# Gate projections of a hybrid decoder layer as three products of hi and lo parts, in 64 filler pieces

## The chip, the core and the metric

One core of a Trainium2 chip runs the whole layer as one program. Its engines are TensorE (PE, with PEld for its weight loads), VectorE (DVE), ScalarE (ACT), GpSimd (POOL) and SyncE (SP, which here only issues DMAs). Each engine runs its own instructions strictly in the order in which they are written, and waits on semaphores for the others; an instruction that waits holds up all that stands behind it on its engine. The metric is the device time of one execution in microseconds, and lower is better.

## What is computed

Input x is 256 tokens by 2048, in fp32. The part of the reference that matters:

```python
h = rms_norm(x)
proj = einsum('btd,dc->btc', h, w_in)          # 2048 x (q,k,v | z | gates)
q, k, v, z, gates = split(proj, ...)           # gates: 2 * 2048 columns
attn = sliding_window_attention(q, k, v)       # 16 heads, 2 blocks of 128 queries
y = rwkv7(z)                                   # 16 heads, delta-rule recurrence
ga, gb = split(gates, (2048, 2048))
merged = sigmoid(ga) * (attn @ w_branch_a) + sigmoid(gb) * (y @ w_branch_b)
x = x + merged @ w_out
x = x + hierarchical_moe(rms_norm(x))          # 32 experts
out = rms_norm(x)
```

## The kernel before

The program runs through these stages: the z, q, k, v and low-rank projections; attention in four units (u = 0 to 3: query block u // 2, and one half of the heads); the recurrence in two halves (hh = 0, 1: eight heads each); the merge with w_branch_a and w_branch_b and the product with w_out; the experts.

The projections ahead of attention, and the merge and w_out behind the recurrence, split both operands. ACT copies a piece of 1024 weight columns into an fp32r buffer (hi), DVE subtracts it from the original (lo), and PE adds three fp32r products, hi by hi, hi by lo and lo by hi (`PRODUCTS`). The gates, 4096 columns of w_in from `GA0` on, are still plain fp32 products. They serve as fillers: PE runs a few of their k steps at places in attention and recurrence where it would wait for DVE or ACT.

`gate_mm(count)` runs the next `count` k steps. A k step multiplies 128 rows of hT by 512 gate columns for 128 tokens, and the compiler makes two PE instructions of it (L571). There are 16 x 16 = 256 of them, 16 for each tile of 128 tokens by 512 columns, and all tiles use PSUM bank 7. `gate_half()` is `gate_mm(8)`. ACT's `gate_out` takes the sigmoid of a finished tile (L1141) and stores it to DRAM (L1143); the next tile's first product waits for it.

The order on PE is written out by hand. Each attention unit has the scores (L595), k steps of the gates, a wait for DVE's softmax (`pr_done`), transposes (L470), 8 more k steps, a wait for ACT's copy of the transposes (`pt_done`, L1157) and the product with v (L615). ACT then copies the result (L1160, `pv_done`), and the next unit's scores wait for that. The four units hold 16, 16, 24 and 24 k steps.

In a half of the recurrence the order on PE is: w and a products (L640, L641, L644), cumulative sums (`cum`, L653), norms (`ks`, L660), transposes of v (`vtr`), bonus (`bon`, L674); then a wait for DVE's long chain up to `bon_done` (L1526 to L1539, with the reciprocal L1527); then L688 and L693 (`l`, `lt`), 8 k steps, L701 (`mt`), more transposes and L717, and five levels of a triangular inverse (L734, k steps, L753, L751). Behind the levels follow L759, the products f, g and rb (L773 to L782), the step between two chunks of the state (`s`, L807), the outputs (`yy`, L818), and the normalisation of y. k steps stand at nearly all of these places: 96 in the first half, 80 in the second.

`ring` has four slots of 2 MB. SP loads gate columns through `load()` into slots as they come free, and w_branch_a and w_branch_b behind them.

The core of the gates before, on PE:

```python
def gate_mm(count):
    for m in range(gate_part[0], gate_part[0] + count):
        tile, k = divmod(m, KT)
        ...
        if k == 0 and tile:
            pe.wait_ge(S("gate_out"), tile)
        if k % 8 == 0:
            full(n)
        last = mm(ps[:, 7, :], hT[:, k, 128 * t:128 * t + 128], slot(n)[:, k % 8, :],
                  start=k == 0, stop=k == KT - 1)
```

Of the kernel before, what the change touches and what calls it, by code (L numbers as in the profile page):

```python
# [4 lines left out]
F32 = mybir.dt.float32  # L5
# [6 lines left out]
P = 128  # L12
# [115 lines left out]
def hybrid_layer(nc, a, out):  # L128
    with ExitStack() as ctx:
# [9 lines left out]

        ring = sb("ring", [P, RING, SLOT])  # L140
# [22 lines left out]

        def over(stack, name, shape, dt=F32R):
            return stack.enter_context(nc.sbuf_tensor(name, shape, dt))

        with ExitStack() as early:
            over(early, "below_w", [P, 15104], F32)
            w3 = [over(early, f"w_{x}", [P, 3, 1024]) for x in ("hi", "lo")]
            w1 = [over(early, f"w4_{x}", [P, 1, 1024]) for x in ("hi", "lo")]  # L170
            over(early, "below_h", [P, 1024], F32)
            h_hi, h_lo = (over(early, f"h_{x}", [P, KT, TOK]) for x in ("hi", "lo"))
# [30 lines left out]
        hT = A(HT, 4096).rearrange("p (k t) -> p k t", k=KT)  # L203
# [59 lines left out]

        def late_pieces(b):

            return [v3[x][:, b, :] for x in range(2)]
# [3 lines left out]
        UZ, UQ, UL, UM, UO = 48, 24, 6, 32, 32  # L270
        BLOCKS = ((0, 0), (0, 1), (1, 0), (1, 1), (0, 2), (0, 3), (1, 2), (1, 3))
# [34 lines left out]
        NG = NL + 2  # L306
        NM = NG + 16
# [28 lines left out]
        def _(sp):  # L336
# [89 lines left out]
        def _(pool):  # L426
# [9 lines left out]
            pool.wait_ge(S("const_in"), 16)  # L436
            for hh in range(HALVES):
# [25 lines left out]
        def _(pe):  # L463
# [95 lines left out]
            def gate_mm(count):  # L559


                for m in range(gate_part[0], gate_part[0] + count):
                    tile, k = divmod(m, KT)
                    b, t = divmod(tile, TT)
                    n = NG + 2 * b + k // 8
                    if k == 0 and tile:

                        pe.wait_ge(S("gate_out"), tile)
                    if k % 8 == 0:
                        full(n)  # L570
                    last = mm(ps[:, 7, :], hT[:, k, 128 * t:128 * t + 128], slot(n)[:, k % 8, :],  # L571
                              start=k == 0, stop=k == KT - 1)
                    if t and k % 8 == 7:
                        last.then_inc(S("chunk_used"), 1)
                    elif k == KT - 1:
                        last.then_inc(S("gate_ps"), 1)
                gate_part[0] += count

            def gate_half():
                gate_mm(8)  # L580
# [7 lines left out]
            for u in range(4):  # L588
# [9 lines left out]
                gate_half()  # L598
                if u >= 2:
                    gate_half()  # L600
# [7 lines left out]
                gate_half()  # L608
# [19 lines left out]
            for hh in range(HALVES):  # L628
# [18 lines left out]
                if hh == 0:  # L647
                    gate_half()
# [6 lines left out]
                last.then_inc(S("half_ps"), 1)  # L655

# [5 lines left out]
                if hh == 0:  # L662
                    gate_half()
# [6 lines left out]
                gate_half()  # L670
# [5 lines left out]
                gate_half()  # L676
                gate_half()
# [18 lines left out]
                gate_half()  # L696
# [31 lines left out]
                for lv in range(1, 6):  # L728
# [8 lines left out]
                    gate_mm((3, 3, 3, 3, 4)[lv - 1])  # L737
# [46 lines left out]
                gate_half()  # L784
# [14 lines left out]
                for c in (1, 2):  # L799
# [10 lines left out]
                    if c == 1:  # L810
                        gate_half()
# [9 lines left out]
                gate_half()  # L821
                gate_half()
# [14 lines left out]
            assert gate_part[0] == 16 * KT  # L837
# [184 lines left out]
        def _(act):  # L1022
# [98 lines left out]
            gate_tile = [0]  # L1121
# [10 lines left out]
            def gate_out():  # L1132

                q = gate_tile[0]
                gate_tile[0] += 1
                b, t = divmod(q, 2)
# [721 lines left out]
```

## Time and profile before

| what | us |
|---|---|
| median of 3 runs | 1860.07 (1857.42 to 1862.98) |
| the profiled execution | 1861.89 |
| its span in the trace | 1860.0 |
| projections ahead of attention | 20 to 247 |
| attention | 247 to 347 |
| first half of the recurrence | 347 to 520 |
| second half of the recurrence | 520 to 693 |
| merge, w_out, router | 693 to 890 |
| experts | 890 to 1860 |

The span is what the trace covers; 1.9 us of the profiled execution lie around it. Times in the trace are microseconds from the start of the span. The rows on which the prediction rests stand below in groups, each with the view that it comes from. In a row of instructions in order of time the first number is the start and the second the duration; the bracket at its end is the engine's idle time ahead of it and what ended it. In a row of a stretch stand its start and end, its length, then busy time and count of instructions of PE, PEld, DVE, ACT and POOL, the mean granted clock as a share of full, the DMA share and GB/s. In a row of a group stand sum and mean (ns) of busy time, then the idle time ahead and what ended most of it.

### The profile page before, as it was taken

To read this page: it belongs to the slowest core of one execution; us is meant where nothing else is said; L and a number is where in the kernel's file an instruction comes from. 1 tells how busy PE (TensorE), PEld (TensorE's weight loads), DVE (VectorE), ACT (ScalarE), POOL (GpSimd) and SP (SyncE) were. 2 spreads that over 40 slices of the span, in tenths; PEclk is the share of its full clock that TensorE was granted. 3 is DMA by queue.
4 is the path that set the end of the run, shared out by engine and by line. 5 is a ranking of instruction groups with operands and counts; after the bars stand their busy time and mean duration, and the time that the engine had idled before them with its cause. 6 is when DMAs were issued, how large, how long until landed. Compare 5 with 4: busy or idle time off the path is not lost.

```text
span 1860.0 us, 24062 instructions
## 1 busy us (share of the span) xinstructions
PE 1454.8 (78%) x10818; PEld 834.8 (45%) x10818; DVE 503.5 (27%) x666; ACT 347.7 (19%) x399; POOL 37.3 (2%) x33
## 2 busy tenths in 40 slices
PE   7999999999989999998767567575575665765754
PEld 7999964447546758886312113122121221211311
DVE  5555444252253256644101001010010100100102
ACT  5444332311121134444101001000010000100001
POOL 1000000002001100000000000000000000000000
PEclk9999999899979999999869779788887888977887
DMA  9555424240202239555699999999999999999993
GB/s 355 189 180 181 143 96 147 95 147 21 97 33 76 99 123 331 196 226 203 274 421 422 422 422 422 422 422 422 422 422 421 422 422 421 422 422 421 423 422 146
DMA packets 114524, 529.04 MB, mean 284 GB/s; under 512 B 7408, under 2 KB 9722, under 8 KB 64410
## 3 DMA queue, kind: packets, MB, share of 16 engines
q1 hardware_dynamic: 109616, 514.50, 69.2%
q0 software_dynamic: 2048, 8.24, 1.2%
q10 hardware_dynamic: 2794, 5.31, 0.8%
q8 instruction: 55, 0.90, 0.2%
q14 instruction: 11, 0.09, 0.0%
HBM read 521.74 MB, written 6.29 MB: 284 GB/s over the span
## 4 chain that ended last, share of the span: by engine, by line
PE 57%; DMA 34%; DVE 4%; ACT 3%; issue 1%; ACTq 0%; DVEq 0%; SPq 0%; POOL 0%; POOLq 0%
DMA ring<-in_expert_w_down 17%; DMA ring<-in_expert_w_up 11%; PE ps L508 11%; PE ps L571 10%; PE ps L843 9%; PE ps L961 7%; DMA ring<-in_expert_w_gate 6%; PE ps L978 5%; PE ps L987 3%; PE ps L930 2%; PE ps L470 1%; PE ps L734 1%; PE ps L751 1%; PE ps L553 1%; PE ps L753 1%
## 5 line engine op out<-in xcount | busy, mean ns | idle before, releaser
L961 PE MATMUL ps<-ring,arena 128*32 128x512 f32 x1280 | 184.7, 729 | 99.9 <-DMA ring<-in_expert_w_up 78.7
L571 PE MATMUL ps<-ring,arena 128*128 128x512 f32 x512 | 232.5, 607 | 3.2 <-ACT rs L1141 3.2
L978 PE MATMUL ps<-ring,arena 128*32 128x512 f32 x768 | 129.6, 836 | 85.6 <-DMA ring<-in_expert_w_down 83.5
L961 PE MATMUL ps<-arena 128*32 128x512 f32 x768 | 124.3, 807 | 76.5 <-DMA arena<-in_expert_w_up 46.2
L508 PE MATMUL ps<-h_hi,w_hi 128*128 128x256 f32 x544 | 155.2, 285 | 4.3 <-DVE w_lo L1399 4.3
L508 PE MATMUL ps<-h_lo,w_hi 128*128 128x256 f32 x544 | 155.0, 285 | 0.0
L508 PE MATMUL ps<-h_hi,w_lo 128*128 128x256 f32 x544 | 154.9, 285 | 0.0
L571 PEld LDWEIGHTS ps<-ring,arena 128*128 128x128 f32 x512 | 96.5, 194 | 118.6 <-issue 111.0
L961 PEld LDWEIGHTS ps<-ring,arena 128*32 128x32 f32 x1280 | 47.1, 130 | 223.5 <-issue 128.7
L1799 DVE TENSOR_TENSOR arena<-arena,ps 128x512 f32<-128x512 f32 x64 | 44.0, 688 | 345.1 <-PE ps L987 345.1
L978 PEld LDWEIGHTS ps<-ring,arena 128*32 128x32 f32 x768 | 31.0, 146 | 178.6 <-DMA ring<-in_expert_w_down 87.9
L508 PEld LDWEIGHTS ps<-h_hi,w_hi 128*128 128x128 f32 x544 | 105.5, 194 | 4.5 <-DVE w_lo L1399 4.5
L508 PEld LDWEIGHTS ps<-h_lo,w_hi 128*128 128x128 f32 x544 | 105.5, 194 | 0.0
L508 PEld LDWEIGHTS ps<-h_hi,w_lo 128*128 128x128 f32 x544 | 105.5, 194 | 0.0
L961 PEld LDWEIGHTS ps<-arena 128*32 128x32 f32 x768 | 28.4, 142 | 166.0 <-issue 73.1
L1491 DVE TENSOR_TENSOR v_lo<-ring,v_hi 128x1024 fp32r<-128x1024 f32 x64 | 78.3, 1225 | 71.0 <-ACT v_hi L1130 70.8
L1289 ACT ACTIVATE arena<-ps 128x512 f32<-128x512 f32 x8 | 4.8, 597 | 450.0 <-PE ps L961 450.0
L1130 ACT ACTIVATE v_hi<-ring 128x1024 fp32r<-128x1024 f32 x64 | 67.6, 1059 | 99.2 <-PE ps L843 99.2
L1776 DVE TENSOR_TENSOR arena<-ps,fnorm 128x512 f32<-128x512 f32 x32 | 22.1, 692 | 231.8 <-PE ps L930 231.8
L1793 DVE TENSOR_TENSOR arena<-arena,ps 128x512 f32<-128x512 f32 x8 | 5.5, 688 | 290.4 <-ACT arena L1289 290.4
L987 PE MATMUL ps<-arena 128*128 128x512 f32 x128 | 68.0, 675 | 16.0 <-ACT arena L1293 16.0
L1399 DVE TENSOR_TENSOR w_lo<-ring,w_hi 128x1024 fp32r<-128x1024 f32 x48 | 58.6, 1224 | 51.7 <-ACT w_hi L1076 51.7
(292 smaller groups left out, 1798.7 us busy)
## 6 DMA issues: line engine op xcount, KB each, us to landing
ring<-in_expert_w_up SPq DMA_DIRECT2D x24, 4096.0 KB, 25.5
ring<-in_expert_w_down SPq DMA_DIRECT2D x24, 4096.0 KB, 23.9
ring<-in_w_in SPq DMA_DIRECT2D x34, 2048.0 KB, 8.2
arena<-in_expert_w_gate SPq DMA_DIRECT2D x16, 4096.0 KB, 23.7
ring<-in_expert_w_gate SPq DMA_DIRECT2D x16, 4096.0 KB, 23.7
arena<-in_expert_w_up SPq DMA_DIRECT2D x8, 4096.0 KB, 16.5
arena<-in_expert_w_down SPq DMA_DIRECT2D x8, 4096.0 KB, 23.4
ring<-in_w_out SPq DMA_DIRECT2D x8, 2048.0 KB, 7.9
```

Of the source, the lines that this page charges most:

```text
L508: last = mm(out, (hi, lo)[w][:, 128 * n:128 * n + 128], hf(x, k), start=start and n == 0 and p == 0, stop=stop and n == 7 and p == 2)
L571: last = mm(ps[:, 7, :], hT[:, k, 128 * t:128 * t + 128], slot(n)[:, k % 8, :], start=k == 0, stop=k == KT - 1)
L843: last = mm(ps[:, bank + t, :], left[x][:, k, 128 * t:128 * t + 128], late_pieces(buf)[w][:, 512 * n:512 * n + 512], start=start and n == ...
L930: last = mm(ps[:, 6 + q % 2, 128 * k:128 * k + 128], hfn[:, t, 512 * q + 128 * k:512 * q + 128 * k + 128], OH[:, 128 * t:128 * t + 128], s ...
L961: last = mm(ps[32 * j:32 * j + 32, u % 2, :], XS[:, k, 32 * j:32 * j + 32], w[:, j, kk, :], start=k == 0, stop=k == KT - 1, tile_position= ...
L978: last = mm(ps[32 * j:32 * j + 32, 2 + nb, :], HIDT[:, kh, 32 * j:32 * j + 32], w[:, j, 512 * nb:512 * nb + 512], start=kh == 0, stop=kh == 3,
L987: mm(ps[:, 6 + u % 2, :], CTB[:, 128 * t:128 * t + 128], YS[:, 512 * nb:512 * nb + 512], start=True, stop=True).then_inc(S(f"b{u % 2}_full ...
L1130: f(late_pieces(y % 3)[0], src, ACT.Copy).then_inc(S("v_hi"), 1)
L1399: v.tensor_tensor(lo, src, hi.bitcast(F32), ALU.subtract).then_inc(S("w_lo"), 1)
L1491: v.tensor_tensor(lo, v_piece(y)[1], hi.bitcast(F32), ALU.subtract).then_inc(S("v_lo"), 1)
L1776: v.tensor_tensor(XS[:, 4 * q:4 * q + 4, :], ps[:, 6 + q % 2, :].rearrange("p (k s) -> p k s", k=4), rep(vec("fnorm", 4 * q, 4), 128), ALU ...
L1799: last = v.tensor_tensor(xs, xs, ps[:, 6 + u % 2, :], ALU.add)
```

## The change

The gates become three fp32r products too. A piece is four k rows of 128 by 256 gate columns, for all 256 tokens: 2 x 4 x 3 = 24 products of 256 columns. There are 64 pieces; four of them make a tile of 256 columns, which fills bank 7 with both token blocks side by side, so there are 16 tiles as before. For each piece ACT makes hi (`g_hi`) and DVE lo (`g_lo`), in place in the ring. They run four pieces ahead of PE: hi of piece p + 4 waits until PE has used piece p. Both are written at fixed places of the ACT and DVE programs (`gates_used`, `used_at`).

The pieces are spread anew, by `ATTN_PARTS` and `HALF_PARTS`: 5, 5, 7 and 7 in the attention units (the pieces ahead of the transposes first, then the one behind them), and 20 in each half of the recurrence.

Slots 0 and 1 of the ring now hold the columns of two tiles, in rows of 1 KB. SP loads tile j when tile j - 2 is used. Slot 2 holds the hi parts. Slot 3 takes a copy of h_lo that POOL makes before attention. w_branch_a and w_branch_b are loaded only when the last gate pieces are used. hT and h_hi move to other places in memory.

```diff
+        UG = 64
+        ATTN_PARTS = ((4, 1), (4, 1), (6, 1), (6, 1))
+        HALF_PARTS = {"cum": 2, "ks": 1, "vtr": 2, "bon": 1, "lt": 3, "level": 1, "f": 1, "s": 1, "yy": 4}
...
-            for c in range(16):
-                load(NG + c, slot(NG + c), cols(GA0 + 512 * (c // 2), c % 2, 512))
+            for j in range(UG // 4):
+                if j < 2:
+                    sp.wait_ge(S("chunk_used"), NL - 1 + j)
+                else:
+                    sp.wait_ge(S("g_used"), 4 * (j - 1))
+                sp.dma_start(ring[:, j % 2, :].rearrange("p (k n) -> p k n", k=KT),
+                             w_in[:, GA0 + 256 * j:GA0 + 256 * j + 256].rearrange("(k p) n -> p k n", p=P))\
+                    .then_inc(S(f"gate_full{j % 2}"), 16)
...
+                if c < RING:
+                    sp.wait_ge(S("g_used"), UG if c else UG - 4)
                 load(NM + c, slot(NM + c), (wa, wb)[c % 2][:, :, 512 * (c // 2):512 * (c // 2) + 512])
...
+            pool.tensor_copy(h_lo2, h_lo[:, :, :]).then_inc(S("h_moved"), 1)
...
             def gate_mm(count):
                 for m in range(gate_part[0], gate_part[0] + count):
+                    j, kq = divmod(m, 4)
+                    if kq == 0 and j:
+                        pe.wait_ge(S("gate_out"), j)
...
+                    pe.wait_ge(S("g_lo"), m + 1)
+                    for t in range(TT):
+                        for k in range(4 * kq, 4 * kq + 4):
+                            for p, (w, x) in enumerate(PRODUCTS):
+                                right = (gate_hi(m), ring_r[gate_raw(m)])[w][:, 256 * (k % 4):256 * (k % 4) + 256]
+                                last = mm(ps[:, 7, 256 * t:256 * t + 256], (h_hi, low)[x][:, k, 128 * t:128 * t + 128], right,
+                                          start=t == 0 and k == 0 and p == 0, stop=t == 1 and k == KT - 1 and p == 2)
+                    last.then_inc(S("g_used"), 1)
...
+            def g_hi(p):
+                j = p // 4
+                if p == 0:
+                    act.wait_ge(S("chunk_used"), NL + 1)
+                if p % 4 == 0:
+                    act.wait_ge(S(f"gate_full{j % 2}"), 16 * (j // 2 + 1))
+                if p >= 4:
+                    act.wait_ge(S("g_used"), p - 3)
+                f(gate_hi(p), ring[gate_raw(p)], ACT.Copy).then_inc(S("g_hi"), 1)
...
+            def gates_used(count):
+                for p in range(gate_part[0], gate_part[0] + count):
+                    if p % 4 == 3:
+                        gate_out(p // 4)
+                    if p + 4 < UG:
+                        g_hi(p + 4)
...
+            def g_lo(p):
+                dve.wait_ge(S("g_hi"), p + 1)
+                v.tensor_tensor(ring_r[gate_raw(p)], ring[gate_raw(p)], gate_hi(p).bitcast(F32), ALU.subtract)\
+                    .then_inc(S("g_lo"), 1)
```

How the instructions stand at three places, in the order of the program, with what they wait for. In the names, arena and ring are the big buffers, ps is PSUM, rs holds the gates' sigmoids. L1161 is hi, L1516 lo, L1171 the gates' sigmoid.

ACT in the first attention unit and into the second, before:

```order
L1151 ACTIVATE arena<-arena 128x8x128 [waits sm_done]
L1152 ACTIVATE aes<-aes 128x8
L1157 ACTIVATE arena<-ps 128x1024 [waits pt_ps]
L1160 ACTIVATE arena<-ps 128x4x128 [waits pv_ps]
L1141 ACT_TABLE_LOAD
L1141 ACTIVATE rs<-ps,rstd 128x512 [waits gate_ps]
```

And now, from the first four hi parts on:

```order
L1161 ACTIVATE ring_r<-ring 128x1024 [waits gate_full0,chunk_used]
L1161 ACTIVATE ring_r<-ring 128x1024 x3
L1198 ACT_TABLE_LOAD
L1198 ACTIVATE arena<-arena 128x8x128 [waits sm_done]
...
L1161 ACTIVATE ring_r<-ring 128x1024 [waits g_used]
L1203 ACTIVATE arena<-ps 128x1024 [waits pt_ps]
L1161 ACTIVATE ring_r<-ring 128x1024 [waits g_used,gate_full0]
L1207 ACTIVATE arena<-ps 128x4x128 [waits pv_ps]
```

A hi part that waits for a load (`gate_full0`, tile 2) now stands ahead of the copy of the unit's result, L1207, the former L1160.

DVE in the recurrence from the end of the chain to the mask products, before:

```order
L1539 TENSOR_TENSOR arena<-ps,arena 128x1024 [waits half_ps,arbk]
L1543 TENSOR_TENSOR arena<-ps,cst 128x1024 [waits half_ps]
L1546 SCALAR_TENSOR_TENSOR arena<-arena,cst 128x1024 [waits x0_done]
L1550 TENSOR_TENSOR arena<-ps,cst 128x1024 [waits half_ps]
L1551 TENSOR_TENSOR arena<-ps,cst 128x1024
L1553 TENSOR_TENSOR arena<-arena,cst 128x1024 [waits lt_done]
L1554 SCALAR_TENSOR_TENSOR arena<-arena,cst 128x1024 [waits dve_step]
L1558 TENSOR_TENSOR arena<-ps,cst 128x1024 [waits half_ps]
```

And now:

```order
L1613 TENSOR_TENSOR arena<-ps,arena 128x1024 [waits half_ps,arbk]
L1516 TENSOR_TENSOR ring_r<-ring,ring_r 128x1024 [waits g_hi] x4
L1619 TENSOR_TENSOR arena<-ps,cst 128x1024 [waits half_ps]
...
L1629 TENSOR_TENSOR arena<-arena,cst 128x1024 [waits lt_done]
L1630 SCALAR_TENSOR_TENSOR arena<-arena,cst 128x1024 [waits dve_step]
L1516 TENSOR_TENSOR ring_r<-ring,ring_r 128x1024 [waits g_hi] x3
L1635 TENSOR_TENSOR arena<-ps,cst 128x1024 [waits half_ps]
```

Four lo parts stand ahead of the first mask product, L1619 (before L1543), and three ahead of the last ones, L1635 (before L1558).

## Rows read from the trace of the kernel before

**Rows 1.** Busy time by stretch: attention, first half, second half of the recurrence.
```profile
257.00:347.00 90.00, 81.59 (x336) 42.04 (x336) 33.48 (x50) 23.60 (x26) 0.00 (x0) 0.98 0.30 106
347.00:515.00 168.00, 161.53 (x1963) 98.88 (x1964) 58.55 (x64) 35.38 (x46) 12.68 (x5) 0.96 0.25 87
515.00:693.00 178.00, 162.47 (x1979) 102.45 (x1977) 76.01 (x83) 41.05 (x50) 13.10 (x6) 0.92 0.23 80
```

**Rows 2.** The chain that ended last: products of 256 columns, and fillers of 16 instructions.
```profile
230.37 16.99 PE ps L553 x144
...
259.83 7.58 PE ps L571 x16
...
280.23 6.87 PE ps L571 x16
...
422.73 2.77 PE ps L571 x6
...
544.21 8.75 PE ps L571 x16
```

**Rows 3.** Groups by line: what hi and lo of a piece cost elsewhere.
```profile
L1130 ACT ACTIVATE v_hi<-ring 128x1024 fp32r<-128x1024 f32 x64 | 67.6, 1059 | 99.2 <-PE ps L843 99.2
L1491 DVE TENSOR_TENSOR v_lo<-ring,v_hi 128x1024 fp32r<-128x1024 f32 x64 | 78.3, 1225 | 71.0 <-ACT v_hi L1130 70.8
```

**Rows 4.** Loads of w_in: KB each, median us from issue to landing.
```profile
ring<-in_w_in SPq DMA_DIRECT2D x14, 2048.0 KB, 8.7
...
ring<-in_w_in SPq DMA_DIRECT2D x1, 1152.0 KB, 5.4
```

**Rows 5.** ACT in order of time: a table load, first and last attention result, a gate sigmoid.
```profile
252.12 1.28 ACT L1151 ACT_TABLE_LOAD   x1
...
268.49 0.60 ACT L1160 ACTIVATE arena<-ps 128x512 f32<-128x512 f32 x1 [7.60 <-PE ps L615]
...
346.74 0.60 ACT L1160 ACTIVATE arena<-ps 128x512 f32<-128x512 f32 x1 [6.88 <-PE ps L615]
...
377.73 0.69 ACT L1141 ACTIVATE rs<-ps,rstd 128x512 f32<-128x512 f32 x1 [1.90 <-PE ps L571]
```

**Rows 6.** DVE in order of time: the softmax of the first unit, first and last.
```profile
249.02 1.67 DVE L1471 SCALAR_TENSOR_TENSOR arena<-cst,ps 128x128 f32<-128x128 f32 x8
...
256.52 1.22 DVE L1483 TENSOR_TENSOR arena<-arena,asum 128x1024 f32<-128x1024 f32 x1
```

**Rows 7.** Clock (third number from the end) without PE work, and in the stretch behind it.
```profile
516.00:520.00 4.00, 0.00 (x0) 0.00 (x0) 3.93 (x6) 0.00 (x0) 0.00 (x0) 0.64 0.00 0
520.00:524.00 4.00, 3.76 (x4) 0.99 (x4) 1.41 (x2) 0.00 (x0) 0.00 (x0) 0.50 0.00 0
```

**Rows 8.** The recurrence in order of time: ACT's norm, then DVE's last of the chain.
```profile
373.50 1.02 ACT L1183 ACTIVATE arena<-ps 128x1024 f32<-128x1024 f32 x1
...
389.14 1.22 DVE L1539 TENSOR_TENSOR arena<-ps,arena 128x1024 f32<-128x1024 f32 x1
```

**Rows 9.** The recurrence in order of time: from the masks to the first level.
```profile
404.58 1.23 DVE L1546 SCALAR_TENSOR_TENSOR arena<-arena,cst 128x1024 f32<-128x1024 f32 x1
...
409.44 3.18 DVE L1554 SCALAR_TENSOR_TENSOR arena<-arena,cst 128x1024 f32<-128x1024 f32 x1
...
422.82 2.34 POOL L443 TENSOR_TENSOR arena<-arena,cst 128x1024 f32<-128x1024 f32 x1 [11.28 <-PE ps L734]
```

**Rows 10.** The chain that ended last: both halves of the recurrence.
```profile
402.09 1.09 PE ps L688 x64
...
420.52 2.21 PE ps L734 x64
...
474.57 7.06 PE ps L571 x16
...
495.96 13.93 PE ps L571 x32
...
569.45 1.09 PE ps L688 x64
```

More of the change, by code:

```diff
@@ L138, in S, with over @@
             return sems[name]
+        def over(stack, name, shape, dt=F32R):
+            return stack.enter_context(nc.sbuf_tensor(name, shape, dt))
+        with ExitStack() as below:
+            ring_r = over(below, "ring_r", [P, RING, SLOT])
         ring = sb("ring", [P, RING, SLOT])
@@ L160, in hybrid_layer @@
         ps = ctx.enter_context(nc.psum_tensor("ps", [P, 8, 512], F32))
-        def over(stack, name, shape, dt=F32R):
-            return stack.enter_context(nc.sbuf_tensor(name, shape, dt))
         with ExitStack() as early:
-            over(early, "below_w", [P, 15104], F32)
+            h_hi = over(early, "h_hi", [P, KT, TOK])
+            over(early, "below_w", [P, 15104 - 4096], F32)
             w3 = [over(early, f"w_{x}", [P, 3, 1024]) for x in ("hi", "lo")]
             w1 = [over(early, f"w4_{x}", [P, 1, 1024]) for x in ("hi", "lo")]
-            over(early, "below_h", [P, 1024], F32)
-            h_hi, h_lo = (over(early, f"h_{x}", [P, KT, TOK]) for x in ("hi", "lo"))
+            over(early, "below_h", [P, 28416 - 23296], F32)
+            h_lo = over(early, "h_lo", [P, KT, TOK])
         with ExitStack() as late:
@@ L562, in gate_mm, with gate_for @@
                 for m in range(gate_part[0], gate_part[0] + count):
[L563 to L576, printed above, removed]
+                    j, kq = divmod(m, 4)
+                    if kq == 0 and j:
+                        pe.wait_ge(S("gate_out"), j)
+                    if m == sum(sum(x) for x in ATTN_PARTS):
+                        pe.wait_ge(S("h_moved"), 1)
+                    low = h_lo if m < sum(sum(x) for x in ATTN_PARTS) else h_lo2
+                    pe.wait_ge(S("g_lo"), m + 1)
[6 more added lines that the diff above has]
+                    last.then_inc(S("g_used"), 1)
                 gate_part[0] += count
-            def gate_half():
-                gate_mm(8)
+            def gate_for(name):
+                gate_mm(HALF_PARTS[name])
             sc = ps[:, 0:4, :].rearrange("p b (j k) -> p (b j) k", j=2)
@@ L655, in _ @@
                 last.then_inc(S("half_ps"), 1)
+                gate_for("cum")
                 pe.wait_ge(S("sq_done"), hh + 1)
@@ L736, in _ @@
                         last.then_inc(S("v1_ps"), 1)
-                    gate_mm((3, 3, 3, 3, 4)[lv - 1])
+                    gate_for("level")
                     if lv == 1:
@@ L1462, in _, with gates_used, used_at @@
             dve.wait_ge(S("small_in"), 16 * 8)
+            gate_part = [0]
+            def g_lo(p):
+                dve.wait_ge(S("g_hi"), p + 1)
+                v.tensor_tensor(ring_r[gate_raw(p)], ring[gate_raw(p)], gate_hi(p).bitcast(F32), ALU.subtract)\
+                    .then_inc(S("g_lo"), 1)
+            def gates_used(count):
+                for p in range(gate_part[0], gate_part[0] + count):
+                    if p + 4 < UG:
+                        g_lo(p + 4)
+                gate_part[0] += count
+            def used_at(name):
+                gates_used(HALF_PARTS[name])
+            for p in range(4):
+                g_lo(p)
             for u in range(4):
@@ L1478, in _ @@
                     .then_inc(S("sm_done"), 1)
+                early = max(0, ATTN_PARTS[u][0] - 4)
+                gates_used(early)
                 dve.wait_ge(S("ex_done"), 2 * u + 2)
@@ L1484, in _ @@
                     .then_inc(S("pr_done"), 1)
+                gates_used(ATTN_PARTS[u][0] - early)
+                gates_used(ATTN_PARTS[u][1])
             dve.wait_ge(S("pv_ps"), 4)
+            dve.wait_ge(S("h_moved"), 1)
             def v_lo(y):
@@ L1540, in _ @@
                     .then_inc(S("bon_done"), 1)
+                for name in ("ks", "vtr", "bon"):
+                    used_at(name)
                 dve.wait_ge(S("half_ps"), half_at("l", hh))
@@ L1570, in _ @@
                                 .then_inc(S(("x_done", "xt_done")[w]), 1)
+                    used_at("level")
                 dve.wait_ge(S("half_ps"), half_at("rb", hh))
```

104 lines of the change are left out of this document (58 added, 46 removed).

## Prediction, made before the changed kernel ran

> **What bounds the kernel now.** I read the stretches first. PE is busy for 81.6 of 90 us in attention, 161.5 of 168 in the first half of the recurrence and 162.5 of 178 in the second, while DVE and ACT reach 58.6 and 35.4 us in the first half [rows 1]. The chain of waits says the same: it runs mostly through PE, and where PE runs fillers, their whole length is on it. Sixteen filler instructions, eight k steps, take 6.87 us [rows 2], so a k step costs 0.859 us and the 256 of them 220 us. A shorter filler can save time only where PE does not then stand still, so the question is what DVE, ACT and the loads do once PE is faster.
>
> **The piece.** The products at L553 have the new shape, 256 columns in fp32r with a new weight load each: 144 in 16.99 us, 0.118 us apiece [rows 2]. The loads hide behind them. I take 0.12 us, so a piece of 24 costs 2.88 us, against 3.44 us for the four k steps that it stands for. Over 64 pieces PE saves 64 x 0.555 = 35.5 us. Each piece adds a hi of 1.06 us on ACT and a lo of 1.23 us on DVE [rows 3], 68 and 79 us in all. Sixteen loads of 2048 KB land 8.7 us after issue now [rows 4]. The new ones have rows of 1 KB; the nearest row is a load of 1152 KB with rows of 1152 bytes, 5.4 us. In proportion to its bytes that would make 9.6 us for 2048 KB, and if part of the 5.4 is fixed, less. I take 8.7, with 7.7 to 9.6 for the range.
>
> The Trainium skill (page "DMA: Bandwidth & Descriptors", section "Anatomy of one DMA") fits a DMA as 2.0 us plus bytes over 436 GB/s, 6.8 us for 2 MB; the trace's 8.7 is slower and decides. With 6.8 the sum below would fall by some 9 us.
>
> A tile's load starts when the tile two before it is used up, and the first hi of that tile stands in ACT's program right behind one further piece. If pieces run back to back, ACT then waits 8.7 - 2.9 = 5.8 us, and all that stands behind it on ACT waits as well.
>
> **Attention.** Before, the first unit's softmax starts on DVE at 249.0 and ends at 257.7, 8.7 us [rows 6]. ACT is free for hi parts at 252.1 [rows 5]. Four hi parts and four lo parts now stand ahead: DVE ends them at 257.8 and the softmax at 266.6. PE can start piece 0 at 254.4 and ends piece 3 at 265.9. The transposes end at 267.7. ACT is busy with the exponential, three hi parts, a table load (1.28 us) and a tile's sigmoid (0.69 us before, taken as 0.9 for two of half width) [rows 5] up to 268.9. Piece 4 waits for that sigmoid and ends at 271.8, the product with v at 272.9. Tile 2's load, issued at 265.9, lands at 274.6; hi(8) ends at 275.7 and the result is copied by 276.3. Before it was done at 269.1 [rows 5]: **+7.2 us**.
>
> In the other three units PE needs the pieces anyway, 5 + 7 + 7 of them, 54.7 us against 55 us before (64 k steps), so nothing is won there. Each of the second and third units again has a hi waiting for a load (tiles 3 and 5) ahead of an ACT copy that PE or the next unit waits for. By the same bookkeeping the second unit ends at 298.6, with hi(12) held until 294.8, and the third at 329.2, with hi(20) held until 327.5. In the fourth, piece 20 waits from 339.9 to 343.6 for a sigmoid that stands behind the exponential, and the unit ends at 360.1, against 347.3 before [rows 5]. So these three cost 83.8 us instead of 78.2: **+5.6 us**.
>
> **Clock.** After 4.5 us without PE work the granted clock fell to 0.64 and then to 0.50 of full, the lower of the two levels, 1.2 GHz [rows 7]. A filler that met the low level took 7.58 and 8.75 us instead of 6.87 [rows 2], 0.7 to 1.9 us more. The new attention has five idle stretches: 6 us at the start, then 3.4, 2.4, 3.7 and 3.5. All five at 1.4 us on the path would make 7 us, none zero. I take **+3.5 us**.
>
> **POOL's copy** of h_lo has four times the elements of L443 (2.34 us [rows 9]), so at most 9.4 us, from about 240 to 249.3. DVE's L1554 took 3.18 us beside POOL's work where L1546, of the same form, took 1.23 [rows 9], so the two can exclude each other. The last mix operations ahead of attention could wait 1.6 us. Between 0 and 1.6 I take **+0.8 us**. The Trainium skill (page "SBUF — State Buffer", section "Who interferes with whom") says that a DVE instruction with two SBUF inputs and a GpSimd instruction that reads SBUF exclude each other for a whole instruction. By that rule it is 1.6 us.
>
> **First half, up to the chain's end.** Twenty pieces take 57.6 us against 96 k steps in 82.5. Before, DVE's chain ran from the end of ACT's norm at 374.5 to 390.4 (15.9 us) [rows 8], and PE came to L688 only at 402.1 [rows 10], 11.7 us after the chain. That surplus can go. The filler between the a and cum products is gone. From the unit's start cum ends after 14.3 us (low clock, as the second half shows), pieces 24 and 25 after 20.1, and the norm is done after 23.4; before it was 27.1. With 15.9 for the chain L688 starts after 39.2 us instead of 54.6 (347.5 to 402.1): **-15.3 us**.
>
> **Masks, in both halves.** Before it is 18.4 us from L688 to the first level (402.1 to 420.5) [rows 10], bound by PE. Now four lo parts stand on DVE ahead of the masks (4.6 us), three more behind L1554, and the last of these, lo(36), needs tile 9. That tile's load is issued 8.6 us after L688 (L688 and L693 in 2.8, then two pieces) and lands at 17.3; hi 18.4, lo 19.6, the last mask products 22.0. PE, which was ready at 15.5, then does its transposes and L717, 4.1 us, and 1.6 more at the low clock that follows 6.5 us of idleness: 27.7 us. **+9.3 us a half**, +18.6 in all. In the second half the pieces stand at the same phase of a tile (20 pieces are five tiles), so its cost is the same.
>
> **Levels.** A filler of six instructions took 2.77 us [rows 2]. The piece takes 2.88 plus some 0.2 for the change of shape: +0.3 four times, -0.5 in the fifth, where eight instructions stood: **+0.7 us a half**. One lo in each level fits in DVE's idle time.
>
> **f, s and yy.** At f and at s 7.06 us become 3.1, and at yy 13.93 become 11.7 [rows 10]. DVE's next work there (under 1 us at s, 9 us at yy) stays shorter than the fillers: -4.0 - 4.0 - 2.2 = **-10.2 us a half**.
>
> **Second half, up to the chain's end.** Before, 49.2 us from 520.2 to L688 at 569.45 [rows 10], with no filler ahead of the norm. Now three pieces' work stands there: the norm is done after 25.7 instead of 22.0 us, and with the chain L688 starts after 41.5: **-7.7 us**.
>
> **The tail.** w_branch loads now start at the last pieces. The first product of the merge came 16.5 us after the last filler; the first slot is loaded by then, and the second is needed 13.8 us after it and lands after 8.7. Nothing. Everything behind moves along: the experts are bound by their loads, whose start depends on the merge's end.
>
> **Sum.** Attention 7.2 + 5.6 + 3.5 + 0.8 = +17.1. First half -15.3 + 9.3 + 0.7 - 10.2 = -15.5. Second half -7.7 + 9.3 + 0.7 - 10.2 = -7.9. Together -6.3 us: 1861.9 becomes 1855.6 in a profiled execution, which lies 1.8 us over the median of 1860.1, and the median becomes **1853.8 us**.
>
> **Rivals.** First, PE stays the bound nearly everywhere: the hi parts reach ACT early enough, because loads land sooner than 8.7 us or ACT's waits fall where nobody needs it. Then attention costs about 5 and the masks 3 a half: 5 - 21.8 - 14.2 = -31 at best, and half of that gain is likelier: 1837. For it speaks that ACT and DVE are idle more than half of the time [rows 1]; against it, that both run in order.
>
> Second, slower: the loads with rows of 1 KB are slow, and every load that holds up ACT passes on its delay. There are five such places (three in attention, one in each mask stage). From -6.3, each microsecond over 8.7 adds 5. The change is slower than before from 10.0 us per load on, by 0.3% from 11.1 us on, and at 12 us the time is 1870.
>
> Third, the low clock takes hold: with all five dips at 1.9 us, and another in each half at the wait for bon_done, it is 6 + 4 us more, 1864.
>
> Fourth, L553's pitch does not hold for pieces: at 0.14 us the pieces cost 31 us more on PE, of which two thirds would show. The shape is the same as L553's, so I give it little.
>
> **Chances.** My sum, give or take 8 us, 0.5; PE stays the bound 0.2; slow loads 0.15; low clock 0.1; a slower pitch 0.05. A difference under 0.3%, 5.6 us, is about what a measurement of this kernel cannot tell from none. Faster by more than that: half of the first and all of the second, and a little more, 0.48; within it 0.3; slower 0.22. The range that should hold 8 times in 10 is 1836 to 1869.
>
> **What would show it.** The pieces, 24 products each, in about 2.9 us; ACT's hi at the start of a tile waiting for ring<-in_w_in, five times with something on the path behind it; attention ending near 360 to 366 instead of 347; L688 of the first half at about 404 us (before 402.1); the first level some 27 us after L688 instead of 18. If DVE's mask products wait for hi by less than 2 us, or the loads land in 7 us, the first rival has it. If the loads show 11 us or more, the second has it.

## The result, and the profile after

| what | before | changed |
|---|---|---|
| median | 1860.72 us (5 runs) | 1870.29 us (5 runs, 1867.80 to 1871.34) |
| ratio | | 1.005, 95% interval 1.0034 to 1.0065 |
| span of the profiled execution | 1860.0 | 1868.4 |
| attention ends | 347.3 | 368.8 |
| merge starts | 693.6 | 699.8 |

The kernel became 0.5% slower; 1853.8 us was forecast, 1869 was the upper end of the range. From here on line numbers of the changed kernel stand for the old ones: L600 is the product of a piece (L571), L1161 a hi part, L1516 a lo part, L1171 the gates' sigmoid (L1141), L1207 the copy of a unit's result (L1160), L709 and L714 the triangular products (L688, L693), L755 the first product of a level (L734), L621 the scores (L595), L1203 the copy of the transposes (L1157), L496 a transpose (L470), L780 the product behind the levels (L759).

First the stretches, with the same columns as [rows 1], cut at the new borders of attention and of the two halves:

```profile
257.00:369.00 112.00, 91.70 (x756) 87.42 (x756) 67.44 (x89) 52.75 (x61) 0.00 (x0) 0.93 0.35 111
369.00:525.00 156.00, 139.47 (x2256) 124.68 (x2256) 82.23 (x85) 53.58 (x67) 13.01 (x5) 0.93 0.26 83
525.00:700.00 175.00, 151.90 (x2295) 132.05 (x2294) 94.99 (x100) 58.97 (x72) 14.12 (x7) 0.92 0.28 95
```

PE is no longer busy all the time. In attention it was idle for 8.4 of 90 us [rows 1] and is now idle for 20.3 of 112, and its mean granted clock fell from 0.98 to 0.93. What took PE's place shows in the chain that ended last. This is its part in the first three attention units (start, duration, what):

```profile
253.74 14.23 PE ps L600 x96
267.98 9.34 DMA ring<-in_w_in
277.35 1.06 ACT ring_r L1161
278.40 0.49 ACT arena L1207
278.94 2.08 PE ps L621 x16
281.02 9.81 PE ps L600 x72
290.85 8.78 DMA ring<-in_w_in
299.65 1.06 ACT ring_r L1161
300.71 0.92 ACT arena L1203
...
303.46 3.61 PE ps L621 x16
307.07 5.99 PE ps L600 x48
...
325.78 8.78 DMA ring<-in_w_in
334.58 1.06 ACT ring_r L1161
335.64 0.49 ACT arena L1207
```

A load of w_in is on the chain three times here. Each time it releases a hi part, and behind that stands a copy that PE waits for. (Where `...` stands, short entries of the chain are left out.) In the mask stage of the first half the same chain reads:

```profile
407.44 1.24 DVE arena L1613
408.81 1.46 PE ps L709 x64
410.27 3.10 PE ps L714 x64
413.37 5.96 PE ps L600 x48
419.35 8.84 DMA ring<-in_w_in
428.20 1.06 ACT ring_r L1161
...
430.43 1.22 DVE arena L1635
```

The second half has the same picture, with 9.08 us of load from 583.11 on. So the chain holds five loads, 44.8 us in all; in the stages of before it held none. The loads themselves are as they were: 2048 KB land in 8.8 us (before 8.7, [rows 4]), only that now somebody waits for them.

### The profile page after: what moved, and what is told of

Read it like the earlier page. It is cut to its first block, busy times and chain, and to the rows that moved or that the text cites. A ratio compares the mean times of both kernels' runs of the same rounds, so it can differ in the third digit from the quotient of the medians.

```text
span 1868.4 us, 26277 instructions
## 1 busy us (share of the span) xinstructions
PE 1439.6 (77%) x11842; PEld 938.9 (50%) x11842; DVE 577.5 (31%) x730; ACT 414.8 (22%) x479; POOL 41.5 (2%) x34
## 3 DMA queue, kind: packets, MB, share of 16 engines
q0 software_dynamic: 2048, 8.24, 1.2%
HBM read 521.74 MB, written 6.29 MB: 283 GB/s over the span
## 4 chain that ended last, share of the span: by engine, by line
PE 57%; DMA 33%; ACT 4%; DVE 4%; issue 1%; ACTq 0%; DVEq 0%; SPq 0%; POOL 0%; POOLq 0%
DMA ring<-in_expert_w_down 19%; DMA ring<-in_expert_w_up 11%; PE ps L534 11%; PE ps L863 9%; PE ps L600 8%; PE ps L981 7%; PE ps L998 5%; PE ps L1007 4%; PE ps L950 3%; DMA ring<-in_w_in 2%; DMA ring<-in_expert_w_gate 1%; PE ps L755 1%; PE ps L772 1%; PE ps L496 1%; PE ps L579 1%
## 5 line engine op out<-in xcount | busy, mean ns | idle before, releaser
L981 PE MATMUL ps<-ring,arena 128*32 128x512 f32 x1280 | 181.1, 717 | 96.6 <-DMA ring<-in_expert_w_up 77.7
L600 PE MATMUL ps<-ring_r,h_hi 128*128 128x256 f32 x1024 | 201.1, 293 | 15.5 <-ACT rs L1171 9.3
L998 PE MATMUL ps<-ring,arena 128*32 128x512 f32 x768 | 143.9, 918 | 75.8 <-DMA ring<-in_expert_w_down 75.1
L981 PE MATMUL ps<-arena 128*32 128x512 f32 x768 | 118.0, 770 | 77.6 <-DMA arena<-in_expert_w_up 40.0
L600 PEld LDWEIGHTS ps<-ring_r,h_hi 128*128 128x128 f32 x1024 | 166.3, 196 | 21.1 <-ACT rs L1171 11.0
L1516 DVE TENSOR_TENSOR ring_r<-ring,ring_r 128x1024 fp32r<-128x1024 f32 x64 | 76.5, 1220 | 66.0 <-ACT ring_r L1161 66.0
L1161 ACT ACTIVATE ring_r<-ring 128x1024 fp32r<-128x1024 f32 x64 | 66.6, 1055 | 131.8 <-PE ps L600 77.2
L600 PE MATMUL ps<-ring_r 128*128 128x256 f32 x320 | 90.5, 283 | 0.0
```

What stands on the lines that cost most here:

```text
L600: last = mm(ps[:, 7, 256 * t:256 * t + 256], (h_hi, low)[x][:, k, 128 * t:128 * t + 128], right, start=t == 0 and k == 0 and p == 0, stop= ...
L981: last = mm(ps[32 * j:32 * j + 32, u % 2, :], XS[:, k, 32 * j:32 * j + 32], w[:, j, kk, :], start=k == 0, stop=k == KT - 1, tile_position= ...
L998: last = mm(ps[32 * j:32 * j + 32, 2 + nb, :], HIDT[:, kh, 32 * j:32 * j + 32], w[:, j, 512 * nb:512 * nb + 512], start=kh == 0, stop=kh == 3,
L1161: f(gate_hi(p), ring[gate_raw(p)], ACT.Copy).then_inc(S("g_hi"), 1)
L1516: v.tensor_tensor(ring_r[gate_raw(p)], ring[gate_raw(p)], gate_hi(p).bitcast(F32), ALU.subtract)\
```

## The experiments

All runs stand beside the kernel before, measured on the same chip at the same time; it took 1860.3 to 1861.4 us. The changed kernel's 1870.29 us stands beside 1860.72. Where a text below names the merge, it is the point at which the chain enters it (693.6 before, 699.8 in the changed kernel).

### One load for each piece

```diff
-            for j in range(UG // 4):
+            for p in range(UG):
...
-                    sp.wait_ge(S("g_used"), 4 * (j - 1))
+                    sp.wait_ge(S("g_used"), p - 7)
```

Each load brings the 512 KB of one piece, and has a semaphore of its own out of eight.

> Edit: each piece of the gates has its own load of 512 KB, issued when the piece that lay in its place two tiles before is used, instead of one load of 2 MB per tile when the whole tile is used. Everything else stays. Theory T (the wait for the whole tile's load, in ACT's queue ahead of copies and in DVE's queue ahead of mask products, is what makes the changed kernel slow): the hi parts no longer wait for a load; attention's four results come about 5, 4, 3.5 and 0 us earlier each, both mask stages 5 to 6 us shorter, and some 3 us of low clock behind the waits go too: 1870.3 falls by 22 to 28 us, to about 1845. Rival R (the cost is the number of hi and lo parts ahead of softmax and masks, or the clock that the new products get, not the loads): less than 5 us less, 1866 to 1870.

Measured: 1841.35 us, ratio 0.9888 (0.9872 to 0.9905), so 28.9 us less than the changed kernel, and faster than before. T had said 22 to 28. No hi part waits for a load any more; the issues by size and median time to landing are:

```profile
ring<-in_w_in SPq DMA_DIRECT2D x64, 512.0 KB, 3.8
```

Attention ends at 354.4, the merge starts at 674.3. The second and third unit need 19.7 and 27.9 us, as they did before (19.7 and 28.5). The rival is out as the cause of the loss: it allowed less than 5 us. But the hi and lo parts are not free. From the first triangular product to the first level e1 still takes 25.1 us in both halves, where it was 18.4 before, and there the chain runs over the lo parts in DVE's queue:

```profile
394.35 4.54 DVE ring_r L1517 x4
...
408.19 2.86 DVE ring_r L1517 x3
```

The Trainium skill (page "DMA: Bandwidth & Descriptors", section "Anatomy of one DMA") gives a fixed part of about 2.0 us and 436 GB/s for a DMA that GpSimd issues; worked out for 512 KB that is an estimate of 3.2 us. The loads here are issued by SyncE: the trace has 3.8, and for 2 MB 8.8 against 6.8 by the same estimate. The trace is slower both times.

### Same loads, other order

In attention, the copies go ahead of the hi part that waits, and its lo part goes behind the next softmax's subtraction:

```diff
                 act.wait_ge(S("pv_ps"), u + 1)
                 f(attnT[...], ps[:, 0, :]..., ACT.Copy).then_inc(S("pv_done"), 1)
+                for p in range(gate_part[0] - late, gate_part[0]):
+                    g_hi(p + 4)
```

> Edit: loads as in the changed kernel. In attention only, ACT copies the transposed probabilities and the result ahead of the hi part that waits for a tile's load (one in the first, third and fourth unit, two in the second), and DVE makes the lo part of it behind the next unit's subtraction of the maximum instead of ahead of the softmax. T: the load is off the path in attention, 4.9 + 4 + 3.5 us and perhaps 2 us of low clock, so 10 to 14 us less than the changed kernel, about 1858; both mask stages keep their 30 us. R: no change of more than 3 us.

Measured: 1857.65 us, 12.6 us less than the changed kernel (ratio to before 0.9981, 0.9971 to 0.9990). Attention ends at 356.3, 12.5 us earlier, the merge starts 12.7 us earlier, and from L709 to the first level it is still 29.9 us. The whole gain lies where T put it.

In the recurrence, the three lo parts go behind the last mask products, the waiting hi part behind the copies:

```diff
-                used_at("lt")
                 dve.wait_ge(S("half_ps"), half_at("mt", hh))
                 v.tensor_tensor(g16(U(10)), mt[:, :, 0, :], tile16(C("mU")), ALU.mult)
                 v.tensor_tensor(g16(U(11)), ...).then_inc(S("mt_done"), 1)
+                used_at("lt")
```

> Edit: loads and attention as in the changed kernel. In both halves of the recurrence, DVE makes the three lo parts of the mask stage behind the last mask products instead of ahead of them, and ACT makes the last hi part of that stage (the one that waits for a load) behind its four copies of transposes. T: from the first triangular product L709 to the first level 30.0 us become 22 to 24 in both halves, 12 to 14 us less in all, about 1857; the wait for the load may come back in part at the fourth level, which needs that piece, 2 us at most. R: no change of more than 3 us.

Measured: 1856.21 us, 14.1 us less (ratio to before 0.9969, 0.9959 to 0.9979). From L709 to the first level it takes 23.1 and 22.9 us instead of 30.0 and 30.1. (In the profiled execution attention, with the same code, took 3.7 us longer than in the changed kernel's, two more stretches at the lower clock; the medians are what counts.) The load has left the chain of this stage; the transposes behind the masks run at full clock again:

```profile
427.06 1.95 PE ps L722 x64
429.03 1.22 DVE arena L1640
430.25 1.14 DVE arena L1641
431.44 1.09 PE ps L496 x8
432.53 2.01 PE ps L738 x64
434.55 1.02 PE ps L496 x8
```

Then both orders together:

> Edit: the changed kernel with the orders of e2 and of e3 together; the loads stay one per tile. If the five places are independent, the gains add: 12.6 + 14.1 = 26.7 us less than 1870.3, about 1844, near e1's 1841 reached by another way. If a wait taken away at one place comes back at the next (ACT still waits for each load somewhere), 5 to 12 us of it is lost: 1849 to 1856.

Measured: 1844.92 us, 25.4 us less (26.7 if they add), with attention at 356.6 and 23.1 us in both mask stages. The places are independent, and a remedy without any change to the loads comes within 4 us of the one that changes them. So the loss came from what stood behind the waiting hi part in the queues; the loads themselves stayed as they were.

### Loads that land later

```diff
+                for c in range(2):
-                sp.dma_start(ring[:, j % 2, :]..., w_in[:, GA0 + 256 * j:GA0 + 256 * j + 256]...)
+                    sp.dma_start(...[:, :, 128 * c:128 * c + 128], w_in[:, GA0 + 256 * j + 128 * c:...]...)
```

> Edit: the changed kernel with each tile's load as two of 128 columns, so that the rows are 512 bytes instead of 1 KB and the tile lands later. The five places in the prediction (first, second and third attention unit, both mask stages) say 5 us more in time for each us that a tile lands later. Estimate of the landing: 10 to 14 us instead of 8.9, so 5 to 25 us slower than the changed kernel. If the loads don't bind (R), 0 to 3 us.

Measured: 1874.73 us, 4.4 us more than the changed kernel (ratio to before 1.0084, 1.0056 to 1.0113; the four executions lie between 1870.5 and 1879.4, so the size of the difference is rough). Rows of half the length cost less than I had estimated: the loads on the chain take 9.3 to 10.7 us. The chain holds the same five loads (the second of each pair):

```profile
268.24 9.56 DMA ring<-in_w_in
291.42 9.42 DMA ring<-in_w_in
328.59 9.32 DMA ring<-in_w_in
423.08 10.74 DMA ring<-in_w_in
587.48 9.41 DMA ring<-in_w_in
```

They sum to 48.5 us against 44.8, 3.6 more. Each starts 0.4 us later besides, because the issue of the pair's first load stands ahead of it, so the data comes some 5.6 us later in all. The stages that hold the loads grew by 7.5 us together: attention by 3.4, the mask stages by 2.7 and 1.4. The rest of the recurrence got 1.6 us shorter, mostly by smaller gaps in the levels (last section), the time from the merge's first transposes to the end 2.5 us, and the span grew by 3.4. In the mask stages a delay of 2.3 and 0.7 us thus came out as 2.7 and 1.4. For attention this is not shown: it grew by 3.4 us for a delay of 2.6, but in e3 the same code took 3.7 us longer with no later load. The slope of the second rival, one for one at five places, fits these figures; only the loads were not slow.

### The clock

```diff
+            def warm(count):
+                for i in range(count):
+                    mm(ps[:, 6, 0:256], h_hi[:, i % 8, 0:128], h_hi[:, i % 8, 0:256], start=True, stop=True)
...
                 gate_for("bon")
+                warm(24)
```

> Edit: the changed kernel with extra fp32r products of 256 columns whose result nobody reads, in PE's long waits: 20 ahead of the first piece, 16 ahead of the waits for the result of the first and third unit and for the copy in the second, 12 ahead of the third unit's last piece, 24 in each half ahead of the first triangular product and 24 ahead of the wait for the mask products. They only replace idle time. If the lower clock that follows each long wait costs what I read (3.1 us of the 14.2 us of the first four pieces, 1 us at each start of scores, 1.7 us at L709 and L714, 1.7 us at the transposes behind the masks), the time falls by 5 to 9 us, to about 1863, and L709 with L714 take 2.8 instead of 4.6 us. If the clock's share on the path is small, within 2 us of the changed kernel; if the extra products outlast their waits, slower by up to 5.

Measured: 1860.92 us, 9.4 us less than the changed kernel, and level with before (ratio 1.000, 0.999 to 1.0009). Work that nobody reads, put into idle time at nine places (one is shown), gave nearly all of the loss back. By stages: attention 2.5 us shorter, the mask stages 2.0 and 2.2, the levels 1.4 and 1.8; the rest nothing or a little more. Not every place gained: the first four pieces still took 14.28 us, because PE stood idle for 3.4 us between the extra products and them, and the 72 products of the second and fourth units 10.31 and 10.24. The places are best seen at the triangular products of the first half. In the changed kernel PE stood idle for 2.43 us ahead of L709; then these products ran 4.56 us. The stretches before and behind (granted clock is the third number from the end):

```profile
404.00:409.00 5.00, 2.57 (x31) 2.40 (x34) 4.93 (x6) 1.74 (x2) 0.00 (x0) 1.00 0.39 135
409.00:413.40 4.40, 4.40 (x129) 4.23 (x124) 4.40 (x5) 0.26 (x1) 0.00 (x0) 0.61 0.01 4
```

With the extra products (L610) ahead of the same two groups, here L722 and L727, the chain reads:

```profile
403.94 2.88 PE ps L610 x24
406.82 1.09 PE ps L722 x64
407.91 1.75 PE ps L727 x64
```

2.84 us, the duration of before [rows 10]. So idleness of 2.4 us, ahead of short products, costs another 1.7 us. In levels the gain is something else: see the last section.

> Edit: the loads by piece of e1 and the extra products of e4 together. Theory T: most of the long waits on PE are gone with the loads, so little of e4's gain of 9.4 us is left to win: 1836 to 1841 against e1's 1841.4. The waits ahead of L709 and behind the mask products are still there in e1, so L709 with L714 and the transposes may still get 1 to 2 us faster in each half. Rival R (low clock is a cost of its own, independent of the waits for loads): again 8 to 10 us less, about 1832. If the extra products now outlast the shorter waits: up to 6 us more.

Measured: 1847.75 us, 6.4 us more than e1. The extra products were sized for the long waits, and with those gone they stand in the way: attention ends at 361.8 instead of 354.4. In the recurrence they still help: from attention's end to the first level 62.1 us instead of 65.2. This run doesn't say what the clock costs in e1; it says that such products pay only where the wait is known. (These stages are read from an execution of 1843.4 us, the fastest of the four; the others took 1847.4 to 1848.6.)

### The spread

```diff
-        ATTN_PARTS = ((4, 1), (4, 1), (6, 1), (6, 1))
-        HALF_PARTS = {..., "lt": 3, ...}
+        ATTN_PARTS = ((3, 1), (3, 1), (5, 1), (5, 1))
+        HALF_PARTS = {..., "lt": 5, ...}
```

> Edit: the changed kernel (one load per tile) with one piece less in each attention unit, 4, 4, 6 and 6 as the k steps stood before, and two more in the mask stage of each half (five instead of three). If the one extra piece in each unit costs what PE needs for it, attention gets 4 x 2.9 = 12 us shorter and each mask stage up to 6 us longer, less where the stage waits for a load anyway (10 us of its 30 are idle on PE): 0 to 10 us less than the changed kernel. If the loads bind in attention, fewer pieces leave less time between a load's issue and its use, and attention gains only 4 to 6 us.

Measured: 1870.43 us, no change from the changed kernel. Attention did get 14.4 us shorter, and the mask stages 3.2 and 5.5 us longer. The rest came back where I had not looked: with four pieces fewer ahead of it, the first half meets the tile's borders at other places. From L780 of the first half to L709 of the second it is 98.4 instead of 89.3 us, because a tile now ends within the outputs, and its sigmoid stands in ACT's queue behind the normalisation of y. ACT in order of time:

```profile
502.71 0.21 ACT L1275 ACTIVATE gn<-gn 128x16 f32<-128x16 f32 x1 [0.19 <-DVE gn L1686]
502.83 1.04 ACT L1161 ACTIVATE ring_r<-ring 128x1024 fp32r<-128x1024 f32 x1
503.89 1.28 ACT L1171 ACT_TABLE_LOAD   x1
505.19 0.84 ACT L1171 ACTIVATE rs<-ps,rstd 128x256 f32<-128x256 f32 x2
```

PE ran the two pieces that finish the tile until 501.4, then stood for 4.72 us until 506.08, before it could start the next one. The two pieces behind that took 8.03 us instead of 5.8, with a granted clock of 0.61 from 506 to 512. That is 7.0 of the 9.1 us. The number of pieces in a stage says little as long as the place of the tile's border isn't looked at.

### A faster version

```diff
-                for name in ("ks", "vtr", "bon"):
-                    used_at(name)
+                g_lo(q)
                 dve.wait_ge(S("half_ps"), half_at("l", hh))
...
+                g_lo(q + 1)
                 dve.wait_ge(S("half_ps"), half_at("lt", hh))
...
-                early = max(0, ATTN_PARTS[u][0] - 4)
+                early = (0, 0, 2, 3)[u]
...
-                gate_for("yy")
+                gate_mm(3 + hh)
```

> Edit: e1, and three changes of order. In the mask stage DVE puts one of its four lo parts ahead of each step instead of all four ahead of the first mask product, and the three lo parts of the stage itself behind the last mask product. In the fourth attention unit the third hi part and the tile's sigmoid go ahead of the exponential. In the first half one of the four pieces at the outputs moves behind the transposes of y, where PE waits for DVE. T: from the end of bon's product to the first level 25.2 us in e1 become 21 in both halves (-8); the fourth unit 32.8 becomes about 30 (-3); the moved piece hides in 4.5 us of idleness (-3) and keeps the clock up for the second half's first products (-2): 16 us less than e1, about 1826. Rival: PE's own work is the bound by now, and the gain is under 6 us.

Measured: 1832.51 us, ratio 0.9849 (0.9831 to 0.9867), 8.8 us less than e1; 16 were expected. The fourth unit takes 30.2 us (32.8 in e1), and the moved piece won 2.9 us at its place and 2.1 in the first products of the second half, all as expected. The mask stage fell short: from L711 (L709) to the first level 23.1 us, where 21 were expected, because the chain now runs mostly through PE there, and L711 and L716 take 4.57 us instead of 2.84 behind 2.5 us of idleness. Some 3 us of the 10.7 that the merge starts earlier are lost behind it.

> Edit: e6 with 20 extra products of 256 columns in each half, in PE's 2.5 us of idleness ahead of the first triangular product L711. If the clock falls because PE stands idle there and what follows pays, L711 and L716 take 2.8 instead of 4.5 us in both halves, 3.4 us less than e6's 1832.5: 1829. If the low clock there has another cause, or what follows isn't on the path, no change.

Measured: 1830.66 us (ratio 0.9845, 0.9822 to 0.9868), 1.9 less than e6. That alone is inside the scatter of both (e6 1829.4 to 1834.2, e9 1829.4 to 1835.1). What the run shows is in the trace: the triangular products are at full clock,

```profile
390.41 2.40 PE ps L612 x20
392.90 1.16 PE ps L716 x64
394.06 1.75 PE ps L721 x64
```

They take 2.91 us instead of 4.57, and in the second half 2.90, with a gap of 0.55 in them, instead of 4.53.

> Edit: e6 with DVE making two of the first four lo parts ahead of the first softmax and two behind its subtraction, where DVE waits for ACT's exponential. The first unit then has PE as its bound (four pieces one behind the other) with softmax 2.3 us earlier but hidden: 0 to 2 us less than e6. If the four lo parts ahead of the softmax were on the path, 2.3 us less.

Measured: 1830.96 us (0.9838, 0.9819 to 0.9858), 1.6 less than e6, inside the scatter too. The softmax of the first unit ends at 264.8 instead of 266.5, but its result comes at 274.3 instead of 273.7: PE's four pieces were the bound. Both versions are 1.6% faster than the kernel before.

## Why the prediction was wrong

The mechanism was right, and in detail: the five loads on the chain are the five places of the text, the pieces take 2.88 us, and e1, e2, e3 and e11 each moved the time as that mechanism says. The sum over it came out at -6.3, the trace has +8.4. Term by term (us; from the chains of both kernels):

| term | predicted | measured |
|---|---|---|
| attention | +17.1 | +21.4 |
| first half, up to L709 | -15.3 | -14.7 |
| its masks | +9.3 | +11.5 |
| its levels | +0.7 | +1.9 |
| f, s, yy | -10.2 | -10.6 |
| second half, up to L709 | -7.7 | -6.3 |
| its masks | +9.3 | +11.7 |
| its levels | +0.7 | +2.4 |
| f, s, yy and the tail | -10.2 | -11.1 |
| merge to end | 0 | +2.2 |

**The step that failed is the clock.** I listed five idle stretches in attention, had rows for 0.7 to 1.9 us at each, and took 3.5 us for all of them. The stretches came, 6.0, 5.9, 3.7, 3.7 and 3.8 us (the third in two parts), where 6, 3.4, 2.4, 3.7 and 3.5 were listed. The second is longer because the first four pieces ran slowly, and tile 2's load was issued at 268.0 and not at 265.9. The chain prices them: 14.23 us for 96 products instead of 11.5; 2.08 and 9.81 instead of 1.1 and 8.6; 3.61 for scores that took 2.02 before; and 10.38 for 72 products in the fourth unit instead of 8.6. That is 2.7 + 2.2 + 1.6 + 1.7 = 8.2 us, 4.7 more than the term, and, less the 0.8 us that POOL's copy did not cost, about the 4.3 by which attention was missed. The granted clock bears it out: 0.55 from 253.7 to 260, 0.50 from 279 to 281, 0.54 from 303.4 to 307.1, 0.60 from 350.7 to 355. One of the five cost nothing: the fourth unit's scores came behind 3.67 us of idleness and took 2.00 us, at a granted clock of 1.00:

```profile
336.17 2.00 PE ps L621 x16
```

The middle between "none" and "all at 1.4" was no reasoned choice: the rows had fillers that met the low level, and none that stayed at full clock behind such idleness. In the masks I had priced the low clock behind the load's wait (1.6 us), but not behind the 2.4 us of idleness ahead of L709, which the piece's own speed had made: 1.7 us in each half. Together that is 8.1 of the 14.7 us between the two sums. e4 shows that such costs are real: filling the waits gave 6.7 us back in attention and masks, and took the triangular products to full clock in both halves. For the pieces of the first, second and fourth unit, 5.6 of the 8.2 us, only the granted clock speaks, since e4 left them slow.

**The levels** were missed by 1.2 and 1.7 us. There the chain has gaps on PE with no releaser, which before had none; why, stays open (last section). The second half's way to L709 was missed by 1.4 us, which I can't account for.

**Merge to end** was taken as a shift. 1.05 us of the 2.2 is in the first products of the experts: 6.29 us for 32 of them instead of 5.24, with a mean granted clock of 0.59 over them, where it had been 0.72. What the other 1.2 are, I can't say; from the merge's first transposes to the end it is 1144.4 us before, 1146.5 in the changed kernel, 1143.6 in e1, 1144.0 in e8 and 1146.9 in e6.

**What was right.** The load at 8.7 us (8.8); the piece (2.88; 3.07 in the levels, for 3.1 predicted); the unwinding of the chain ahead of L709, 39.2 and 41.5 predicted, 40.1 and 42.9 measured; f, s and yy; the masks' 27.7 us, which make 29.4 with the 1.7 of clock, against 30.0 and 30.1 measured. POOL's copy was bounded by 9.4 us and taken as +0.8. It took 3.60 us, from 239.2 to 242.8, and nothing on the chain waited for it. The rule of the Trainium skill (page "SBUF — State Buffer", section "Who interferes with whom") that I weighed for it has its effect elsewhere: DVE's L1630 took 3.21 us beside POOL's L469. In e6, where another DVE operation stands beside POOL, that one takes 3.43 us, and L1639 (the former L1630) 1.22. The trace agrees with the page, and shows that an order on DVE chooses which instruction pays.

**The rivals.** The third, the low clock, is what happened, and I gave it 0.1. Its price for the clock was nearly right, and the sum should have used it: 9.5 us for the five dips in attention (8.2 measured) and 4 for the wait for bon_done, which is the idleness ahead of L709 (3.4 measured). It came to 1864 and not to 1870 because the levels, the second half's way to L709 and the time from the merge on were short in it as in the sum. The first, PE bound everywhere, did not happen: the hi parts did wait. Its 1837 does not follow from its own working either: half of 31 us is 1844.6. e1 took the load waits away and came to 1841 us, but with DVE's lo parts on the chain of the mask stages, so that number is no proof of it. The second had the wrong load time; its slope fits e8.

## What to carry to other kernels

A filler that is made faster, but now needs a load and two more engines, adds instructions to their queues; look at what stands behind the one that waits for the load. Load in the units in which a buffer is used up (here 512 KB for each piece instead of 2 MB for each tile: 29 us), or put the waiting instruction behind those that others wait for (25 us without touching a load). And price every idle stretch that a change makes on TensorE twice: once as the wait, once for the clock behind it, with the rows of work that met the low level. The second price is not always paid: one stretch of 3.67 us here cost nothing.

## What the hardware showed that I had not expected

The clock can fall after shorter idleness than I had thought: 2.43 us without work ahead of L709, and the following 4.4 us had a mean granted clock of 0.61, so most of them were at the lower of the two levels, 1.2 GHz. It need not fall: behind 3.67 us ahead of the fourth unit's scores it was still 1.00. With 20 products in the idleness ahead of the triangular products it stayed at 1.00, as e9 shows:

```profile
390.00:396.00 6.00, 5.91 (x154) 5.56 (x153) 5.63 (x7) 1.06 (x1) 0.00 (x0) 1.00 0.34 90
```

PE also stood still with nothing to wait for that the profile shows, in the middle of a group of products. The chain in the fourth level of the first half of the changed kernel:

```profile
465.35 0.69 PE ps L755 x22
466.04 1.11 issue
467.15 1.49 PE ps L755 x42
```

There are three such gaps, 1.11, 0.85 and 1.57 us. In 460 to 470 the trace has a w_in load of 2 MB (10.1 us to landing, the slowest of all) and two transfers of the queue that it calls "instruction". Such transfers also stand where there is no gap, three of them from 445 to 460. e2, e3, e7 and e11 have a gap of 1.6 us at a level's first product too, e8 one of 0.8, e1, with small loads, one of 0.62, and before and e4 none in the levels. Of the others with small loads, e6 has one of 0.48, e9 one of 0.80 in a level of the first half, e10 one of 0.58. That instructions arrive late beside a large load would fit the shorter gaps of e1, e6 and e10; but e9's is no shorter than e8's, and e4 has the large loads and no gap. No run was made to tell, and the cause stays open.
